# Input projection of three heads as pairs of tiles and token halves, in seven products for eight

## The reference

```python
xn = rmsnorm(x, norm_gain)
proj = einsum('btd,dp->btp', xn, w_in)
gb, gc, hc, zc, q, k, v, o, zm, ig, fg = split(proj)
yc, conv_new = short_conv(gc * hc, conv_buf, conv_w)
y_conv = gb * yc * silu(zc)
h, state = mlstm_seq(q, k / sqrt(128), v, ig + b_i, log_sigmoid(fg + b_f), state)   # chunks of 128
y_m = rms(h) * mh_gain * sigmoid(o) * silu(zm)
out = x + einsum('btw,wd->btd', concat([y_conv, y_m]), w_out)      # then a final rmsnorm
```

## Time and profile before

| | us |
|---|---|
| median of three runs | 1103.91 (1102.55 to 1104.18) |
| profiled execution, span | 1100.9 |
| PE busy | 1061.1 (96%) |
| DVE busy | 540.9 (49%) |
| ACT busy | 340.7 (31%) |
| POOL busy | 257.9 (23%) |

### The profile page before, as it was taken

One profiled execution on the slowest core, in us unless ns is written; L12 is line 12 of the kernel. 1 busy time (PEld: TensorE's weight loads), 2 busy tenths in 40 slices (PEclk: granted clock), 3 DMA queues, 4 the chain that ended last, 5 costly groups with the idle time before them and its releaser, 6 DMA issues. The chain is left out here.

```text
span 1100.9 us, 17978 instructions
## 1 busy us (share of the span) xinstructions
PE 1061.1 (96%) x7180; PEld 602.0 (55%) x7180; DVE 540.9 (49%) x1008; ACT 340.7 (31%) x672; POOL 257.9 (23%) x333
## 2 busy tenths in 40 slices
PE   3999999999999999999999999999999999999995
PEld 3655546565666555656665556566655555444442
DVE  5786664556553434575534345655332323434333
ACT  6636434243402232434022324340213131111111
POOL 5012313021211323212113232121111121542422
PEclk9999999999999999999999999999999999999998
DMA  9484532033200322342003224310212062365651
GB/s 243 135 182 78 132 86 49 24 107 101 89 22 17 96 63 77 93 110 89 21 17 96 64 77 120 102 32 22 93 43 86 25 220 91 108 223 205 233 201 77
DMA packets 124184, 108.74 MB, mean 99 GB/s; under 512 B 42384, under 2 KB 109092, under 8 KB 124100
## 3 DMA queue, kind: packets, MB, share of 16 engines
q1 hardware_dynamic: 88192, 68.83, 22.0%
q0 software_dynamic: 7600, 25.03, 6.2%
q10 hardware_dynamic: 28308, 13.73, 4.8%
HBM read 65.43 MB, written 33.41 MB: 90 GB/s over the span
## 5 line engine op out<-in xcount | busy, mean ns | idle before, releaser
L800 PE MATMUL bank<-xTh,Wh 128*128 128x512 f16 (+2 forms) x1304 | 421.2, 342 | 5.7 <-DVE Wl L163 5.7
L801 PE MATMUL bank<-xTl,Wh 128*128 128x512 f16 (+2 forms) x1304 | 423.9, 342 | 0.0
L802 PE MATMUL bank<-xTh,Wl 128*128 128x512 f16 (+2 forms) x1304 | 423.6, 342 | 0.0
L802 PEld LDWEIGHTS bank<-xTh,Wl 128*128 128x128 f16 x1304 | 129.2, 99 | 120.3 <-issue 0.7
L800 PEld LDWEIGHTS bank<-xTh,Wh 128*128 128x128 f16 x1304 | 129.2, 99 | 113.4 <-DVE Wl L163 6.0
L801 PEld LDWEIGHTS bank<-xTl,Wh 128*128 128x128 f16 x1304 | 129.3, 99 | 108.8 <-issue 2.4
L809 PE MATMUL bank<-Wh,xTh 128*128 128x128 f16 x544 | 92.8, 219 | 0.6 <-DVE ysum L163 0.6
L811 PE MATMUL bank<-Wh,xTl 128*128 128x128 f16 x544 | 92.8, 219 | 0.0
L810 PE MATMUL bank<-Wl,xTh 128*128 128x128 f16 x544 | 92.8, 219 | 0.0
L163 ACT ACTIVATE tz<-bank 128x512 f32<-128x512 f32 x32 | 19.1, 598 | 148.4 <-PE bank L802 147.7
L672 POOL TENSOR_TENSOR ysumst<-ysum,ysumst 128x1024 f16<-128x1024 f32 x16 | 34.1, 2130 | 105.5 <-ACT ysumst L163 105.5
(11 more groups left out here) (336 smaller groups left out, 1520.5 us busy)
## 6 DMA issues: line engine op xcount, KB each, us to landing
wst<-in_w_in ACTq DMA_DIRECT2D x23, 512.0 KB, 3.9
xs<-in_x_prompt SPq DMA_DIRECT2D x22, 512.0 KB, 4.3
y_ops<-ysumst POOLq DMA_DIRECT2D x16, 512.0 KB, 3.2
w_ops<-xs SPq DMA_DIRECT2D x16, 448.0 KB, 4.5
wst<-in_w_in SPq DMA_DIRECT2D x13, 512.0 KB, 5.5
out<-xs POOLq DMA_DIRECT2D x11, 512.0 KB, 2.9
Wh<-y_ops SPq DMA_DIRECT2D x12, 448.0 KB, 3.6
Wl<-y_ops SPq DMA_DIRECT2D x12, 448.0 KB, 4.4
```

Source lines behind the costliest of these rows:

```text
L800: mm(out, wh[:, k, :], xh, start=(k == 0), stop=False)
L801: mm(out, wh[:, k, :], xl, start=False, stop=False)
L802: last = mm(out, wl[:, k, :], xh, start=False, stop=(k == KT - 1))
```

## The change

Head 0 stays as it is. In heads 1 to 3 four pairs of tiles, (Q,K), (GC,HC), (GB,ZC), (O,ZM), take the place of eight single tiles. A pair is a 2 x 2 product: two halves of the 1024 inputs, two tiles, and the block's tokens in two halves of 256. Seven products of sums and differences (P1 to P7, Winograd's form) take the place of eight, each 4 k-steps x 3 matmuls of 256 columns. Their sums need copies in between: `first_taken`, `second_taken`, `third_taken` and `c21_out_to` on ACT (256 columns of a bank), three additions on DVE.

The operands: of each block's tokens three raw parts and four sums stand in DRAM (`x_ops`, seven operands of 512 KB), and ACT loads them into a ring of ten places. SP stores the raw parts in head 0 (`store_raw`, 12 DMAs per block); the sums come from eight "pairs" of loads, made by ACT (`scale_pair`, `high_pair`), POOL (`pair_differences`), DVE (`low_pair`), four turning DMAs and four stores each, pairs 0 to 3 in head 0 and pairs 4 to 7 in (1,1) and (1,2). The weights' gain and sums are made by POOL (`unit_gain`, `unit_sum`), their high parts by ACT, the low parts by DVE. The slabs move to (2,1), (2,2), (3,1), (3,2), and ACT copies each chunk's result out of its bank (`number_taken`).

```diff
-SLAB_FIRST = {(1, 1): 0, (1, 2): 2, (2, 1): 4, (2, 2): 6}
+SLAB_FIRST = {(2, 1): 0, (2, 2): 2, (3, 1): 4, (3, 2): 6}
...
+            def product_of(q, i):
...
+                if i == P6:
+                    pe.wait_ge(taken_out, p1_taken(q))
...
+                if i == P7:
+                    pe.wait_ge(taken_out, u2_taken(q))
+                if i == P4:
+                    pe.wait_ge(taken_out, u3_taken(q))
+                if i == P3:
+                    pe.wait_ge(added_up, c22_added(q))
+                begins, x, w = i in (P1, P5, P2), xops[x_slot(later, i)], wop[p]
+                for k in range(4):
...
+                    mm(out, wh, xh, start=(begins and k == 0), stop=False, skip_group_check=not begins)
+                    mm(out, wh, xl, start=False, stop=False, skip_group_check=not begins)
+                    last = mm(out, wl, xh, start=False, stop=(k == 3), skip_group_check=not begins)
+            def head_block(g, b):
+                q = pair(g, b)
+                product_of(q, P5)
...
+                product_of(q, P6)
+                product_of(q, P2)
+                product_of(q, P7)
+                product_of(q + 1, P1)
+                heads_turn(g, b)
+                product_of(q, P4)
...
+                product_of(q, P3)
+                product_of(q + 1, P5)
+                arguments(g, b)
...
+                values(g, b)
...
+                product_of(q + 1, P6)
+                product_of(q + 1, P2)
...
+                keys_turn(g, b)
...
+                product_of(q + 1, P7)
...
+                scores(g, b)
...
+                product_of(q + 2, P1)
...
+                product_of(q + 1, P4)
+                product_of(q + 1, P3)
...
+            def act_head_block(g, b):
...
+                second_taken(q)
+                third_taken(q)
...
+                if (g, b) == (1, 1):
+                    scale_pair(5)
+                first_taken(q + 1)
...
+                heads_high(g, b, t0(g, b, "hT"))
+                c21_out_to(q, kf[:, 0:HALF])
+                if last_of_head:
+                    for i in range(3):
+                        unit_high_of(g + 1, KQ, i)
...
+                exponents(g, b)
+                values_taken(g, b)
+                second_taken(q + 1)
+                sums_high(g, b)
...
+                if last_of_head:
+                    for i in range(2):
+                        unit_high_of(g + 1, VV, i)
+                third_taken(q + 1)
+                if (g, b) == (1, 1):
+                    high_pair(5)
+                if (g, b) == (1, 2):
+                    high_pair(7)
...
+                first_taken(q + 2)
...
+                if (g, b) in SLAB_FIRST:
+                    output_high(SLAB_FIRST[g, b])
...
+                second_taken(q + 2)
...
+                if b == NB - 2 and g < H - 1:
+                    if g == 1:
+                        act.wait_ge(sums_out, SUMS_OUT * 8)
+                    else:
+                        act.wait_ge(wo_out, 32 * (SLABS // 2))
+                    load_unit(act, g + 1, KQ)
+                    load_unit(act, g + 1, VV)
...
+            def store_raw(b):
...
+                for op, k0, half in ((X_11, 0, 0), (X_21, KT // 2, 0), (X_22, KT // 2, 1)):
+                    for h in range(2):
+                        for part in range(2):
...
+                            sp.dma_start(dst, xT[:, b, part, k0:k0 + KT // 2, at:at + P]).then_inc(raw_out, 16)
```

More of the change, by code:

```diff
@@ new lines, with t0, t1, pair @@
+T0_AT, T0_END = places(T0_PRO, t0_uses, t0_later)
+T1_AT, T1_END = places(T1_PRO, t1_uses, t1_later)
+def t0(g, b, name, first=False):
+    return T0_AT[g, b, name]
+def t1(g, b, name, first=False):
+    return T1_AT[g, b, name]
+def pair(g, b, p=0):
+    return 4 * (NB * (g - 1) + b) + p
+def made(q, i):
+    if i == P1:
+        return 7 * q - 1 if q else 1
+    step = 7 * q + {P5: 2, P6: 3, P2: 4, P7: 5, P4: 7, P3: 8}[i]
+    return step - 1 if q == PAIRS1 - 1 and i in (P4, P3) else step
+def p1_taken(q):
+    return 4 * q if q else 1
@@ new lines, in build, with x_set, x_sum @@
+        sets = {"first": arena[:, 0:8192].bitcast(F32), "second": arena[:, 8192:16384].bitcast(F32)}
+        x_sets = {name: [a[:, i * D:(i + 1) * D] for i in range(4)] for name, a in sets.items()}
+        x_sets["rows"] = [x[:, :] for x in xs] + [xmore[:, :]]
+        x_sets["weights"] = [f for f in flat] + [hz[:, 0:D]]
+        X_SET = ("first", "first", "second", "rows", "weights", "rows", "weights", "rows")
+        def x_set(m):
+            return x_sets[X_SET[m]]
+        def x_sum(m, i):
+            x = x_set(m)
+            return (x[2][:, 0:BT], x[2][:, BT:D], x[1][:, 0:BT], x[0][:, BT:D])[i]
@@ L704, in pool_block @@
-                for unit in ((), (14,), ())[b] if first else ():
-                    x_power(unit)
+                if b == 2:
+                    pair_differences(1)
+                if follows:
+                    pair_differences(3)
+                    unit_gain(1, VV)
+                if b:
+                    store_sums(g, b - 1)
+                for unit in ((), (14,), (), ())[b]:
+                    x_power(unit)
+                if b == 1:
+                    pair_differences(0)
@@ L818, in use_t1, with gates @@
                 pe.wait_ge(t1_free, count)
-            def gates(units, tok, n, count):
+            def gates(units, parts, n, count):
                 for unit in units:
@@ L996, in _ @@
+            pe.wait_ge(consts, CONST)
             pe.wait_ge(par_in, 16 * 3)
```

1509 lines of the change are left out of this document (1243 added, 266 removed).

## The result

The changed kernel takes 1261.8 us (median of four runs, 1260.4 to 1262.8), the kernel before 1103.4 in the same runs: 1.143 times the time, interval 1.142 to 1.145. The profiled execution spans 1260.4 us, against 1100.9 in the earlier trace rows; 159.5 us have come.

What follows compares the result with a forecast made beforehand. PE was taken to bound the kernel, busy 1061.1 of 1100.9 us. Terms: 1103.9 - 57 (columns) + 7 (F) + 22 (B) + 11 (A) + 13 (C) + 14 (D) + 11 (E) + 8 (G) = 1133 us; range 1075 to 1168.

Steps and rivals of the forecast that it cites:

- E: Head 0: raw stores on SP delay the token turns and so the gates; 11 us, between 3 and 26.
- Columns, -57: Heads 1 to 3, 12 blocks: 336 matmuls of 256 columns replace 192 of 512, saving 57 us (55 to 62).
- A: End of (2,2): scalar engine waits for slab stores before issuing loads, second_taken behind; 11 us (5 to 14).
- B: Blocks (1,3), (2,3): POOL's gains and sums for the next head delay the copies; 22 us for both (10 to 26).
- C: (2,1) and (3,1): slab high parts wait for POOL ahead of second_taken; 6.5 us each, 13 (6 to 15).
- D: (1,1) and (1,2): token pairs' high parts wait for POOL ahead of first_taken; 14 us (8 to 18).
- F: Every block: copy before the second pair's P7 comes about 1 us late in 7 blocks; 7 us (0 to 16).
- G: Whole kernel: PE's clock drops to half after waits, nine of 5 us and more; 8 us (0 to 15).
- Rival 3: Heads 1 to 3: a 256-column matmul doesn't cost half of a 512-column one; about 1190 us, chance 0.05.
- The two rules: Skill rules: 256-byte stores in head 0 below line rate, sum 1144; POOL and vector engine share a port, sum 1140.
- Rival 1: Heads 1 to 3: POOL's work is done in time, so the waits behind it vanish; 1079 us, chance 0.27.
- Rival 2: More than counted: small-piece stores hold head 0's turns, clock falls after each wait, block copies wait longer; 1160 and above, chance 0.10.

Runs made afterwards that it cites:

- noraw: Against the changed kernel, the 48 stores of raw parts in 256-byte pieces left out, products reading a stored sum instead; 1253.1 us.
- nounits: Against the changed kernel, loads, gains, sums and splits of the weights of heads 2 and 3 left out; 1200.9 us.
- bare: Against the changed kernel, the token pairs and the weight preparation of heads 2 and 3 left out together; 1128.2 us.
- feedless: Against the changed kernel, token pairs, all heads' weight preparation, raw stores and mixed difference left out, token slots loaded from on-chip memory; 1094.6 us.
- bzwait: Against the changed kernel, POOL waits for the block's gate product before head 1's BZ gain in head 0's last block; 1262.8 us.

## Why the prediction was wrong

**Where the miss lies.** The sum had 11 us for head 0 (E) and, from its end on, 18: the columns' -57, 67 for A to D and F, 8 for G. Measured are 65.6 and 94. So, by the spans, 55 us of the miss lie in head 0 and 76 behind it: 48 of idle time of PE (115 for 67), 20 of the clock (27.5 for 8) and 8 that aren't placed.

**Columns, -57: right in price.** The matmuls of a product start 0.109 apart, and blocks with the least extra work take 47.9 to 50 ((2,2), which was named as one without any, carries two slabs). With the feeding left out, (1,2) gains 3.6 and (1,3)+(2,0) 4.0 a block for the 4.74 of the sum, the difference being the values' copy that PE now waits 1.0 for. The bounds of this term were added up wrongly: 0.111 and 0.108 give 51 and 63, not 55 and 62; that doesn't change the outcome. Rival 3, columns that are not halved, is out.

**E, head 0: the first step that failed.** It gave 11 us, with 3 and 26 as ends, and named its own limit, 20; head 0 ends 65.6 later. I walked one queue, SP's, and priced what I found there, the raw stores. Those are some 9 (noraw): the three waits at the gates came much as forecast (3.25, 4.97 and 2.66 for 5, 3 and 2.5), though the stores are the cause of the first and the third alone, and twelve issues in a row took 6.8 to 15.9 us on SP, not 5. What I left out is the rest of the change in head 0: the mixed difference on POOL ahead of the norms (7.5), ACT's pair scalings and its waits for loads and stored sums (8.2 at 218.82; others at the end of the head), the token pairs as a whole (41 with all that they draw), and the weights of head 1 ahead of (1,0). I had asked "how long does the queue take", where each instruction put into an engine's order has to be asked what it waits for and who waits behind it. The same walk that found A to D in heads 1 to 3 wasn't made for head 0, where DVE and ACT were busier (56.74 and 41.65 us of the 100 in the first window above, 51.57 and 33.52 in the second).

**Heads 1 to 3: the second.** The walk had the right kind of wait and too few places. Of the 24 waits behind the mark, eight, 46 of the 97.7 us, are at the places of A to D. Of the other 52 us, 26 are in the first blocks of the heads, which weren't walked (5.30, 4.71 and 2.42 in (1,0), 4.32 and 2.42 in (2,0) and in (3,0)); 7 at copies of the chunks' results behind ACT's loads of stored sums (4.96 and 2.34); 5 at the start of (1,3); 6 in the rounds of the sample states; 7 are smaller ones in (1,3) and (2,3).

**G, the clock: mis-sized.** 8 forecast, with 15 at the most; 48 measured (49.8 us of busy time lost, before 1.7). The mechanism was named and the number of waits was too small: I counted nine, and there are 34 more of 2 us and above than before. About 20 of the 48 lie in head 0.

**A, the start of (2,3): right.** 11 forecast, a wait of 12.13. The same loads at the start of (1,3) were missed. There the stored sums, which they wait for instead of slabs, were in time; the four issues themselves held ACT for 6.8 us (rows above) and PE for 4.82, and nounits got 8 back there.

**B: right in place, too small.** 11 a block; the wait at P4 came as forecast (5.17 in both blocks), the other, at the second pair's P7, did not. In its place came three smaller ones (1.8 to 2.6) and, at the start of the next head, one of 4.3 at the mixed values. From 566 to 630 us, in and behind (1,3), PE has 15.6 us of idle time and loses 1.4 to the clock, and nounits got 20 back with the first block of the next head.

**C, the slabs: right.** 6.5 each forecast; 5.88 and 6.89, with 0.77 at a later product. They stay in bare and feedless, as they should.

**D: too small by half.** 14 forecast; without the pairs (1,1) and (1,2) get 29 back. At the third pair's P6, where the walk put most of it, only (1,2) has a wait (2.62 at 524.97). The turn of the keys, just ahead of the second P7, waits 4.00 and 4.06 where 1 to 2.6 were forecast; the 4.96 and 2.34 behind the loads of stored sums the walk didn't have.

**F: mis-sized.** 7 forecast, up to 16. feedless has 35 us of idle time from the mark on beyond that of before, of which C is 14: some 20 for what every block has, and it is in other copies than the second P7's (the values' copy, the state round).

**The two rules.** The raw stores cost 9 us with their 256-byte pieces and landed in 3.0 us for 128 KB, against 2.2 for a store of that size in the earlier trace rows. But in the changed kernel the other stores of that size landed later still, from its page (KB each, median us from issue to landing):

```profile
x_ops<-arena SPq DMA_DIRECT2D x48, 128.0 KB, 3.0
y_ops<-yst POOLq DMA_DIRECT2D x16, 128.0 KB, 4.6
```

The Trainium skill ("DMA: Bandwidth & Descriptors", section "Specifications") has such pieces below line rate; no run here shows or refutes it, and E's upper end, 26, which I hung on it, didn't come. On B the observation of bzwait bears: DVE's 128x4 product at 4.35 beside POOL's gain and at 0.16 without. The Trainium skill ("SBUF — State Buffer", section "SBUF: two separate sides") has the two engines share a port that one of them locks for a whole instruction. The trace agrees that one waits for the other, but the wait lasted through two instructions of POOL: one meeting cost 4 us, not the 0.7 that I had estimated.

**Rivals.** Rival 1, POOL in time, fell: B, C and D have their waits, though not each at its place. Rival 2, more than counted, is nearest to what came, by the clock and by F, but not by the stores that it named first. Its chance, 0.10, was too small for a sum of which most unknown terms could only grow; and each term had its end worked out alone, though waits and clock grow together.

What stays open: how much of the 134 us that sums and units cost (bare) an order could hide. The orders tried got 38 us back in all, 29 of them in head 0.

## What to carry to other kernels

A change that saves columns on a full engine pays with work on the others, and here that work was paid less by its busy time than by its place: each new instruction, in every stage that gets one, needs its wait and the list of those behind it, on all queues and not on the one that looks busiest. Price the bare saving first (here 9 us with almost nothing feeding it, from 57 by columns): it is what is left to win as long as the waits that stay without the feeding, here the slabs' and those on the copies, are not mended too. Where one walk is made for one stage, make it for all of them before adding up.

## What the runs showed of the hardware

A short product on the vector engine, 128x4 elements, took 4.35 us while POOL ran two products of 128x1024, and 0.16 when POOL waited; the overlap then stretched the next work of both (5.79 for 2.56, 4.72 for 3.76). Every wait of PE of 4 us and more in the changed kernel's rows above was followed by a granted clock of 0.50, the lower of two levels, for some 3 to 7 us: 142 us at that level in all, against 11 before. And ACT, issuing four loads of weights and states early in block (0,3), was held by the issues themselves, as at 550.22 above. Its timeline in the changed kernel:

```profile
269.66 3.36 ACTq L595 DMA_DIRECT2D wst<-in_w_in  x3
273.06 5.15 ACTq L625 DMA_DIRECT2D cs<-in_state_mlstm_c  x1
278.31 0.60 ACT L266 ACTIVATE kf<-bank 128x512 f32<-128x512 f32 x1 [8.48 <-issue]
```

I had put it down to SP's twelve raw stores, issued at the same time; without them it is still 7.16, so they are not its cause (at 550.22 the last of them lay 260 us back), and what is stays open.
